# One 8 KB gather per expert instead of two of 4 KB, in a ring of six slots, with the expert weights formed on ScalarE

## The reference, cut to what matters

```python
def chunk(args):
    xc, ec, gc = args
    u_sel = u_tab[ec]
    act = jax.nn.gelu(jnp.einsum('tkd,td->tk', u_sel, xc), approximate=False) * gc
    return jnp.einsum('tk,tkd->td', act, v_tab[ec])
...
x = x + g2 * _peer(h, pk_w_q[i], pk_keys[i], pk_u[i], pk_v[i])
```

## Time and profile before

| | |
|---|---|
| median of 3 runs | 3542.96 us (3541.77 to 3545.4) |
| the profiled execution, its own time | 3545.07 us |
| its span in the trace | 3543.3 us |
| granted TensorE clock, mean share of full speed | 0.921 |
| busy: PE, PE weight load, DVE | 90%, 65%, 71% |
| busy: ACT, POOL | 14%, 35% |
| moved by DMA | 957.18 MB, mean 270 GB/s |

### The profile page before, as it was taken

The page is one execution under the profiler, slowest core; times in us unless marked ns, Lnnn a source line. Parts: engine busy times, 40 slices in busy tenths (PEclk is TensorE's granted clock), DMA queues, the critical chain, the costliest instruction groups (busy, mean ns, idle before and its releaser), DMA issues.

```text
span 3543.3 us, 44528 instructions
## 1 busy us (share of the span) xinstructions
PE 3179.2 (90%) x12852; PEld 2291.5 (65%) x12852; DVE 2502.8 (71%) x5303; ACT 479.0 (14%) x1062; POOL 1254.0 (35%) x1168
## 2 busy tenths in 40 slices
PE   7899869699999999999979897838999999999996
PEld 3685746596776766555568784737877676655554
DVE  0397899778888886666623586397788888766665
ACT  0211211010000000000043215201100000000001
POOL 0000000105555557777500000002255555677773
PEclk9899979659999999999979999975699999999998
DMA  8234315319999999999922340213399999999996
GB/s 313 87 133 170 114 64 180 131 32 388 410 403 409 406 406 410 410 410 410 372 84 97 118 143 12 85 59 100 114 410 407 406 401 409 405 410 410 410 410 262
DMA packets 242900, 957.18 MB, mean 270 GB/s; under 512 B 26953, under 2 KB 27129, under 8 KB 225146
## 3 DMA queue, kind: packets, MB, share of 16 engines
q0 software_dynamic: 147456, 536.94, 38.5%
q1 hardware_dynamic: 95354, 419.17, 31.2%
HBM read 953.90 MB, written 2.10 MB: 270 GB/s over the span
## 4 chain that ended last, share of the span: by engine, by line
PE 53%; DMA 16%; issue 12%; DVE 11%; ACT 4%; POOL 3%; DVEq 0%; POOLq 0%; ACTq 0%; SPq 0%
DMA v_rows<-in_pk_v,idx_now 14%; PE out_e L727 13%; PE acc L718 13%; PE acc L488 11%; PE mid L708 6%; PE acc L480 4%; DVE mod_rows L1290 2%; POOL v_rows L426 1%; DVE scratch L1309 1%; POOL u_rows L420 1%; DMA u_rows<-in_pk_u,idx_now 1%; PE mid L679 1%; PE out_e L510 1%; DMA weights<-in_ada 1%; DVE scratch L1306 1%
## 5 line engine op out<-in xcount | busy, mean ns | idle before, releaser
L727 PE MATMUL out_e<-weights,mod_rows 128*128 128x512 f32 x2048 | 932.4, 598 | 61.6 <-DVE mod_rows L1335 59.7
L718 PE MATMUL acc<-h_t,weights 128*128 128x256 f32 x4096 | 933.8, 381 | 0.0
L718 PEld LDWEIGHTS acc<-h_t,weights 128*128 128x128 f32 x4096 | 784.0, 192 | 217.8 <-issue 123.5
L426 POOL DMA_INDIRECT v_rows<-in_pk_v,idx_now x512 | 630.5, 1231 | 606.0 <-DVE mod_rows L1290 484.9
L1290 DVE SCALAR_TENSOR_TENSOR mod_rows<-v_rows,acts,mod_rows 128x1024 f32<-128x1024 f32 x512 | 657.9, 1285 | 199.0 <-DMA v_rows<-in_pk_v,idx_now 195.5
L1273 DVE SCALAR_TENSOR_TENSOR u_rows<-u_rows,h_rows 128x1024 f32<-128x1024 f32 x512 | 625.8, 1222 | 82.5 <-DMA u_rows<-in_pk_u,idx_now 81.7
L727 PEld LDWEIGHTS out_e<-weights,mod_rows 128*128 128x128 f32 x2048 | 377.2, 190 | 468.1 <-issue 368.0
L420 POOL DMA_INDIRECT u_rows<-in_pk_u,idx_now x512 | 564.6, 1103 | 292.4 <-issue 142.3
L415 POOL COPY idx_now<-pick_idx 128x8 int32 (+1 forms) x128 | 56.2, 439 | 1348.2 <-DVE pick_gate L1268 1300.5
L708 PEld LDWEIGHTS mid<-scratch 128*128 128x128 f32 x2048 | 338.6, 257 | 20.2 <-DVE scratch L1309 16.9
L708 PE MATMUL mid<-scratch 128*128 128x64 f32 x2048 | 341.4, 343 | 10.6 <-DVE scratch L1309 10.6
(11 more groups left out here) (184 smaller groups left out, 2072.0 us busy)
## 6 DMA issues: line engine op xcount, KB each, us to landing
weights<-in_u_t SPq DMA_DIRECT2D x256, 512.0 KB, 6.7
weights<-in_pk_v SPq DMA_DIRECT2D x256, 512.0 KB, 6.7
weights<-in_ada SPq DMA_DIRECT2D x42, 1024.0 KB, 4.9
weights<-in_pk SPq DMA_DIRECT2D x32, 1024.0 KB, 4.8
weights<-in_w_qkv SPq DMA_DIRECT2D x24, 1024.0 KB, 4.8
weights<-in_w_in SPq DMA_DIRECT2D x16, 1024.0 KB, 4.8
weights<-in_w_out SPq DMA_DIRECT2D x8, 1024.0 KB, 4.9
u_rows<-in_pk_u,idx_now POOLq DMA_INDIRECT x512, 10.9
```

The lines of the kernel that those rows point to most:

```text
L426: nc.gpsimd.indirect_dma_start(v_rows[:, r % VR, :], None, a["pk_v"], bass.IndirectOffsetOnAxis(ap=idx_now[:, 1, par, r:r + 1], axis=0)).t ...
L718: last = nc.tensor.matmul(acc[s][:, 0:HALF], weights[:, s, k * P:(k + 1) * P], h_t[:, k, :], start=k == 0, stop=k == KB - 1)
L727: last = nc.tensor.matmul(out_e[2 * tt + c][:, :], e_act[:, s, tt * P:(tt + 1) * P], weights[:, s, D + c * 512:D + (c + 1) * 512], start=F ...
```

## The change

The tables `pk_u` and `pk_v` are laid out side by side on the host as one table `uv`, whose row holds an expert's `u` and then its `v`, 8 KB. One indirect DMA per pick brings both. They land in a ring `rows` of six slots of 8 KB per partition; the 8 + 4 places of 4 KB are gone (the room is the same, and every other tile that shared it is laid over the ring instead). A slot now stays taken from the landing of the row through `u_dot` until `v_add` has read its second half. The dense `v` blocks are read from the second halves of the same table, 4 KB of every 8 KB.

The batches are gone: `u_dot` of the two picks of block b+1 stands in block b, before the two `v_add` of block b. So in a block DVE now does: line 1335's multiplication, one-hots if there are any, `u_dot`, `u_dot`, `v_add`, `v_add`. In `row_acts`, ACT takes the Gelu of two dot products and multiplies each with its gate (an activation Copy with the gate as scale), in each block; the multiplication on DVE is gone. POOL's lists hold 12 picks. The unrolling of the loops changes with it (12 blocks a turn). Before the stage, two `u_dot` follow the last one-hots, instead of eight spread among them. Where the dense products are started, nothing changes.

```diff
-UR = 8
-VR = 4
-BATCH = 8
+SLOTS = 6
+BODY = 12
+LIST = 12
...
-        u_rows = sb("u_rows", [P, UR, D])
-        v_rows = sb("v_rows", [P, VR, D])
+        rows = sb("rows", [P, SLOTS, 2 * D])
...
-                    sp.dma_start(weights[:, s, D:2 * D], a["pk_v"][bass.ds((i + l * NK) * NK, NK), :]).then_inc(vtab_in[s], 16)
+                    sp.dma_start(weights[:, s, D:2 * D], a["uv"][bass.ds((i + l * NK) * NK, NK), D:2 * D]).then_inc(vtab_in[s], 16)
...
+            def row(l, n, r, par, at):
+                if l or type(n) is not int or n >= SLOTS:
+                    pool.wait_ge(row_used, n + (l * ALL_PICKS + 1 - SLOTS))
                 steps.apart()
-                nc.gpsimd.indirect_dma_start(u_rows[:, r, :], None, a["pk_u"], bass.IndirectOffsetOnAxis(
-                    ap=idx_now[:, 0, par, r:r + 1], axis=0)).then_inc(u_in[r], 16)
+                nc.gpsimd.indirect_dma_start(rows[:, r, :], None, a["uv"], bass.IndirectOffsetOnAxis(
+                    ap=idx_now[:, par, at:at + 1], axis=0)).then_inc(row_in[r], 16)
+
+            def some(l, tile, first, count, par, offset):
+                n = first + (tile * PICKS + l * ALL_PICKS)
+                if type(first) is not int or n:
+                    pool.wait_ge(row_used, n - 4)
                 steps.apart()
+                steps(nc.gpsimd.tensor_copy(idx_now[:, par, 0:count], pick_idx[:, tile, bass.ds(first, count)]))
+                for j in range(count):
+                    row(l, first + (tile * PICKS + j), (offset + j) % SLOTS, par, j)
...
-            def row_gelu(q, b):
-                act.wait_ge(dots_ready, b + (q * BATCHES + 1))
-                at = bass.ds(b * BATCH, BATCH)
-                nc.scalar.activation(acts[:, at], dots[:, at], ACT.Gelu).then_inc(gelu_ready, 1)
+            def row_acts(l, tile, b):
+                n = b * 2
+                act.wait_ge(dotted, n + (l * ALL_PICKS + tile * PICKS + 2))
+                steps(nc.scalar.activation(acts[:, bass.ds(n, 2)], dots[:, bass.ds(n, 2)], ACT.Gelu))
+                for j in range(2):
+                    one = bass.ds(n + j, 1)
+                    last = nc.scalar.activation(acts[:, one], acts[:, one], ACT.Copy, scale=pick_gate[:, 1, tile, one])
+                last.then_inc(acts_ready, 1)
...
+                    for j in range(count):
+                        b = first + j
...
+                        dve.wait_ge(e_gelu_ready, b + (dense_no(l, g) + 1))
+                        tt_op(e_now, e_now, gate, ALU.mult).then_inc(e_act_ready, 1)
+                        if g == 0 and j % 2 == 0:
+                            hots(1, group + j // 2, j // 2 % 2)
+                        for e in range(2):
+                            n = at + 2 + e
+                            if not end or j < count - 1:
+                                u_dot(l, g, b + 1, e, k(n), n % SLOTS)
...
+                        for e in range(2):
+                            v_add(l, g, b, e, (at + e) % SLOTS)
```

More of the change, by code:

```diff
@@ new lines, in _ @@
+            for l in range(DEPTH):
+                pool.wait_ge(picks_ready, 4 * l + 4)
+                pool.wait_ge(scores_full, PK[l, 1] + 8)
+                some(l, 0, 0, LIST, 0, 0)
+                with steps.loop(PICKS // BOTH - 1, 2) as i:
+                    for n in range(2):
+                        some(l, 0, i * BOTH + LIST * (n + 1), LIST, 1 - n, 0)
+                some(l, 0, PICKS - 20, LIST, 1, 0)
+                some(l, 0, PICKS - 8, 8, 0, 0)
+                some(l, 1, 0, 4, 1, 2)
+                with steps.loop(PICKS // BOTH, 2) as i:
+                    for n in range(2):
+                        some(l, 1, i * BOTH + (LIST * n + 4), LIST, n, 0)
+                some(l, 1, PICKS - 4, 4, 0, 0)
@@ L1008, in peer, with blocks @@
                     for s in range(2):
[L1009 to L1026, removed]
+                        take_gates(0, i * 2 + s, s)
+                row_acts(l, 0, 0)
+                def blocks(g, first, count, group=0, end=False):
+                    for j in range(count):
+                        b = first + j
+                        act.wait_ge(e_dots_full, b + (dense_no(l, g) + 1))
+                        nc.scalar.activation(e_act[:, j % 2, :], acc[j % 2][:, 0:HALF], ACT.Gelu).then_inc(e_gelu_ready, 1)
+                        if g == 0 and j % 2:
+                            take_gates(1, group + j // 2, j // 2 % 2)
+                        if not end or j < count - 1:
+                            row_acts(l, g, b + 1)
+                        elif g == 0:
+                            row_acts(l, 1, 0)
+                times = ROUND // BODY
+                with steps.loop(times, BODY) as i:
+                    blocks(0, i * BODY, BODY, i * (BODY // 2))
+                blocks(0, times * BODY, ROUND - times * BODY, times * BODY // 2, True)
+                blocks(1, 0, 2)
+                with steps.loop(times, BODY) as i:
+                    blocks(1, i * BODY + 2, BODY)
+                blocks(1, times * BODY + 2, 2, 0, True)
             def ada(l):
@@ L1319, in peer, with blocks @@
[L1319 removed]
+                for e in range(2):
+                    u_dot(l, 0, 0, e, 0, e)
+                def blocks(g, first, count, turn, group=0, end=False):
+                    for j in range(count):
+                        b = first + j
+                        at = 2 * j if type(first) is not int else 2 * (first + g * ROUND + j)
+                        k = (lambda n: turn + n // SLOTS) if type(first) is not int else (lambda n: n // SLOTS)
+                        e_now = e_act[:, j % 2, :]
+                        if g == 0:
+                            gate = region[:, bass.ds(b * HALF + SPARE * HALF, HALF)]
+                        else:
+                            gate = gates_1[:, :, bass.ds(b, 1), :]
+                            e_now = e_now.rearrange("p (q r) -> p q r", r=QUAD).unsqueeze(2)
+                        dve.wait_ge(e_gelu_ready, b + (dense_no(l, g) + 1))
[4 more added lines that the diff above has]
+                            n = at + 2 + e
+                            if not end or j < count - 1:
+                                u_dot(l, g, b + 1, e, k(n), n % SLOTS)
+                            elif g == 0:
+                                u_dot(l, 1, 0, e, k(n), n % SLOTS)
+                        for e in range(2):
+                            v_add(l, g, b, e, (at + e) % SLOTS)
```

163 lines of the change are left out of this document (51 added, 112 removed).

## The result

The change makes the kernel slower: 3660.96 us (3652.11 to 3673.07, 4 runs) against 3544.12 us before, a ratio of 1.0333 with a 95% interval of 1.03 to 1.0366. I had forecast 3528.5 us, within 3500 to 3575. The profiled execution took 3665.38 us, 120.3 more than the one before.

A forecast was written before the change was run, and what follows sets the result against it. The full DMA pipe was taken to bound the second half of each expert stage, TensorE the first. 3545.07 - 16.1 (packets) + 1.6 (ACT) = 3530.6 us for the profiled execution, 3528.5 against the median; range 3500 to 3575.

The forecast's parts named there:

- The ring of six: Expert stages' row slots: hold T + 3.6 us, 11.5 us left for issue and landing, some 1.9 to spare; cost 0.
- The ring runs dry: Rival, at POOL's list change and pairwise slot release: 3553 us if only the uncovered part counts, 3621 if all; chance 0.14.
- POOL's list change: Every six blocks POOL stops 2.9 us, covered by dense loads in line: 0; uncovered, up to 0.17 us a block.
- Packets: Second half of the stages: half as many packets, of 8 KB, save 0.134 us a block over 120 blocks, -16.1 us.
- The sum of -16.1: Total packet gain in the second halves: 60 blocks in each layer, 120 x 0.134 us.
- DVE: Expert stages: loses `weigh`, gains some 0.2 us a block from dependent `v_add`, hidden in idle time: 0.
- ACT: Three small instructions a block, about 1 us, hidden; not hidden at a stage's first block, 0.8 us a layer: +1.6 us.
- The dense loads starve: Rival, expert stages: dense loads behind 8 KB gathers land in 10.4 us; at 12.5, +154 us; chance 0.07.

The follow-up runs named there:

- four slots, late dots: late_dots with a ring of four slots instead of six: 3817.5 us, ratio 1.077 to the kernel before.
- alternate: The changed kernel with DVE's order in a block back to `u_dot`, `v_add`, `u_dot`, `v_add`: 3543.82 us, ratio 1.0007 to the kernel before.
- alt_lists: alternate, with POOL also copying the next index list after the sixth row of the current one: 3540.67 us, ratio 0.9987 to the kernel before.
- late_dots: The changed kernel with both `u_dot` of a block's picks at the start of that same block, not in the block before: 3538.92 us, ratio 0.999.
- late_two_4k: late_dots with each slot filled by two gathers of 4 KB rows instead of one of 8 KB: 3558.57 us, ratio 1.0045 to the kernel before.
- before_pairs: The kernel before the change, with both `u_dot` ahead of both `v_add` in a block: 3541.53 us, ratio 0.9994.
- dve_weighs: The changed kernel with the multiplication by the gates back on DVE and only the Gelu on ACT: 3676.28 us, ratio 1.039 to the kernel before.
- late_lists: late_dots, with POOL also copying the next index list after the sixth row of the current one: 3539.56 us, ratio 0.9981 to the kernel before.

## Why the prediction was wrong

**The sign.** The step that failed is "The ring of six": "the pipe stays full: 0". Its method was right and two of its terms were not. I put the hold at T + 3.6 us. Measured, it is 13.0 us at T = 7.97, so T + 5.0. Of the 1.4 us more, 1.2 is DVE waiting for the second row of a pair (2.35 us on the average before the second `u_dot` of a block, which lengthens the hold of one slot in two), with both slots of the block before still held behind it. I had listed DVE's wait at `u_dot` and the order of the four instructions, each alone, and did not put the one into the other. And I put the room that is needed at 10.9 to 11.5 us. What the change took is 2T = 3.6 + 1.4 + 11.05, so T = 8.0. A full pipe was seen only with a room of 12.7 us and more (the steps are DVE's):

| second half, layer 0 | hold | room | GB/s | us a block |
|---|---|---|---|---|
| four slots, late dots | 6.1 | 11.5 | 358 | 8.8 |
| the change | 13.0 | 11.1 | 392 | 7.97 |
| alternate | 10.1 | 12.9 | 413 | 7.61 |
| alternate, early lists | 10.0 | 12.7 | 417 | 7.51 |
| late dots | 5.7 | 17.0 | 417 | 7.48 |

The room in this table is what a run took and no fixed need: 11.5 us stands beside 358 GB/s and 11.1 beside 392. But at 7.5 us a block the order of the change leaves 15.0 - 5.0 = 10 us, less than any run took. The rival "The ring runs dry" was therefore the case, at its full price and above: I had 8.02 us a block in both halves and 3621 us; it was 7.97 to 8.05 in the second and 8.17 to 8.28 in the first. That its 8.02 fits the second half is luck: it was made of the list stop alone, which is worth half of the loss. What makes the first half slower still is open. Its hold is no longer than the second's (12.5 us in either layer), but its room is: 12.0 and 12.2 us. The row that spoke for it, 12.5 us of landing in a full pipe, I set aside with the 8.9 of the first half; but there too a `v` slot had 14.3 us of room by the trace.

**"POOL's list change", put at 0.** Wrong: 56 us. The cover I named, dense loads in line, lasted until 1508 and not to 1510. It is 3 to 5 us where the room is enough (alt_lists), so it is part of the same cause. The copy itself took 1.26 us in the stretch shown, where I had 0.78.

**"Packets".** Right in kind and size: 417 against 410 GB/s, 0.13 us a block for 0.134, shown by late_dots against late_two_4k. The Trainium skill's 3 cycles a packet ("DMA: Bandwidth & Descriptors", section "Why small descriptors are slow"), an estimated 0.06 us a block, is less than half of what is measured. Whether the rest is packets or completions stays open: no run separates them.

**The sum of -16.1.** Even with room it was 4 us and not 16 (late_dots). The gain a block was sized right; what was wrong is the 60 blocks a layer that I gave it to, and that I read the steps from line 1335, which is DVE's. DVE entered the second half 4.3 us ahead of `v_block` (1289.37 against 1293.64) and at block 60 `v_block` came right behind it, so TensorE's own step was (1747.99 - 1293.64) / 60 = 7.57 us and not 7.64. These are the starts of `v_block` of blocks 16 and 60 in the kernel before, then of blocks 0, 16 and 60 in late_dots:

```profile
1410.28 3.70 PE L727 MATMUL out_e<-weights,mod_rows 128*128 128x512 f32 x8 [0.94 <-DVE mod_rows L1335]
...
1747.99 3.70 PE L727 MATMUL out_e<-weights,mod_rows 128*128 128x512 f32 x8 [1.21 <-DVE mod_rows L1335]
```

```profile
1292.15 3.60 PE L716 MATMUL out_e<-weights,mod_rows 128*128 128x512 f32 x8
...
1411.67 3.69 PE L716 MATMUL out_e<-weights,mod_rows 128*128 128x512 f32 x8
...
1743.74 3.69 PE L716 MATMUL out_e<-weights,mod_rows 128*128 128x512 f32 x8
```

| `v_block`, second half of layer 0 | before | late_dots |
|---|---|---|
| blocks 0 to 16, together | 116.6 | 119.5 |
| blocks 16 to 60, each | 7.68 | 7.55 |
| blocks 60 to 63, together | 17.3 | 18.5 |

Where the pipe is full in both kernels, late_dots gains 5.6 us in 44 blocks. It gives 2.9 back in the first 16 and 1.2 in the last three, which leaves 1.6; in layer 1 it is 3.6 by the same reckoning, 5 us in all. Before the change, part of what a full pipe costs was paid out of work done ahead, and the ring starts and ends with less of that. That it is the ring that has less ahead is argued; the rows show only where the time is, and late_two_4k, with 4 KB gathers, loses it in the same places.

**"DVE" and "ACT".** Hidden, as put: before_pairs and dve_weighs bear it out. The 1.6 us at the start of a stage is 0.6: from ACT's row Gelu to the first product with the gates it is 1.14 us (791.06 to 792.20), where it was 0.83 (791.73 to 792.56), and the same in layer 1.

**"The dense loads starve".** Not in the change, where they land after some 8 us and TensorE waits for line 1327. In late_dots what this rival described is there in kind: 11.1 us of landing, for which I had put 10.4, and 11.3 as the time there is at the pipe's pace. Each block's weights come just in time, from a pipe that moves 417 GB/s. Whether a third place for `weights` would bring more than that, no run shows.

## What to carry to other kernels

Of a ring, write down the whole cycle: slots over rows per block, times the block, is hold plus room, and the hold counts every wait that stands between the first use and the last on the engine that frees the slot, above all waits for the next rows. Merging two transfers with different lifetimes gives each the longer one, and the bytes in flight fall though the bytes of buffer don't; move the first use next to the last, or alternate uses and releases, before you pay for more slots. And measure a full stage by the engine that ends it, not by one that runs ahead, and the gain of a faster pipe only over the blocks in which it is full.

## What the runs showed of the hardware

- Gathers of 8 KB rows, mixed 2 to 1 with dense loads of 4 KB rows, fill the pipe at 417 GB/s; with 4 KB rows it is 410. The dense loads among them then land 11.1 us after their issue (median), where it is 6.7 among gathers of 4 KB rows (late_dots, late_two_4k).
- A gather's issue on POOL took from 0.93 to 1.98 us for the same shape, and its copy of 12 indices from 0.20 (late_lists, at 1523.82) to 1.26 us. And four times in the changed kernel, 108 gathers apart, there is a gap of 1.3 to 2.6 us in front of a gather, with no wait that the profile shows:

```profile
1230.31 1.42 POOL L417 DMA_INDIRECT rows<-in_uv,idx_now  x1 [7.22 <-DVE mod_rows L1284]
1234.36 1.43 POOL L417 DMA_INDIRECT rows<-in_uv,idx_now  x1 [2.63 <-issue]
```

  It recurs in late_dots, at the same four gathers. Its cause is open.
